# Value rows between the two page items of a slot, and the dot ahead of the score evacuation, in a decoder step on one core

## The reference, cut to what matters

```python
    s2 = jnp.einsum('btghd,btgnld->btghnl', q, ks).astype(jnp.float32) * scale      # selected scores
    o_slc = jnp.einsum('btghk,btgkd->btghd', p2.astype(vs.dtype), vs.reshape(...))   # selected values
...
    act = jax.nn.gelu(jnp.einsum('thkd,td->thk', u_tab[experts], xc))                # the dots
    v = v_tab[experts]
    return jnp.einsum('thk,thkd->td', (gate * act).astype(v.dtype), v)               # the value rows
```

## Time and profile before

| | |
|---|---|
| median of 3 runs | 2478.64 us (2475.55 to 2478.97) |
| the profiled execution | 2483.12 us, its span 2481.3 us |
| TensorE, matmul | 1764.9 us, 71% of the span |
| VectorE | 1271.6 us, 51% |
| ScalarE | 355.4 us, 14% |
| POOL | 847.4 us, 34% |
| DMA | 961.24 MB, mean 387 GB/s |
| granted TensorE clock, mean | 0.797 |

### The profile page before, as it was taken

How to read it: one execution, slowest core, us unless ns; L and a number is a source line. 1 busy time by engine, 2 the same in 40 slices (tenths; PEclk the granted TensorE clock), 3 DMA queues, 4 the chain that set the end, 5 groups by cost and what they waited for, 6 DMA issues and landing times.

```text
span 2481.3 us, 29990 instructions
## 1 busy us (share of the span) xinstructions
PE 1764.9 (71%) x9899; PEld 969.1 (39%) x9899; DVE 1271.6 (51%) x2384; ACT 355.4 (14%) x805; POOL 847.4 (34%) x595
## 2 busy tenths in 40 slices
PE   8999999979997787878665656769533333455335
PEld 6777766544696565556412213218200000000000
DVE  0500121253588775556959362345778754454651
ACT  0001110331230011110201020022200011021111
POOL 0000000000013443344324142332465677767662
PEclk9999999999998998889887778979655555555556
DMA  9999989997499999999999999999999999999997
GB/s 382 369 359 363 367 327 380 377 356 288 170 415 355 404 405 409 406 407 407 402 390 400 363 376 407 420 421 420 420 422 417 421 421 422 422 421 421 422 422 319
DMA packets 213309, 961.24 MB, mean 387 GB/s; under 512 B 23841, under 2 KB 89378, under 8 KB 122754
## 3 DMA queue, kind: packets, MB, share of 16 engines
q0 software_dynamic: 84432, 626.26, 61.4%
q1 hardware_dynamic: 92914, 300.39, 31.3%
q10 hardware_dynamic: 35808, 32.65, 3.9%
HBM read 952.73 MB, written 14.88 MB: 390 GB/s over the span
## 4 chain that ended last, share of the span: by engine, by line
DMA 46%; PE 39%; DVE 5%; issue 4%; ACTq 4%; POOL 1%; SPq 1%; ACT 1%; POOLq 0%; DVEq 0%
DMA sb<-in_peer_v,sb 24%; PE bank L1110 14%; DMA sb<-in_nsa_t 12%; PE bank L1531 6%; DMA sb<-in_peer_u,sb 5%; PE bank L1806 4%; PE bank L1417 3%; PE bank L1464 3%; PE bank L1181 2%; DMA sb<-in_nsa_v 2%; DVE sb L2480 2%; ACTq L440 2%; PE bank L1209 2%; DMA sb<-in_w_out 1%; DMA sb<-in_a_v 1%
## 5 line engine op out<-in xcount | busy, mean ns | idle before, releaser
L1806 PE MATMUL bank<-sb 128*32 128x512 f32 x2304 | 470.4, 867 | 495.8 <-DMA sb<-in_peer_v,sb 464.0
L2590 POOL DMA_INDIRECT sb<-in_peer_v,sb x288 | 497.3, 1727 | 576.1 <-PE bank L1806 510.9
L2480 DVE CUSTOM_DVE_ANT_1 sb<-sb 128x2048 f32<-128x2048 f32 x192 | 439.8, 2293 | 320.6 <-DMA sb<-in_peer_u,sb 317.4
L2590 POOL DMA_INDIRECT sb<-in_peer_u,sb x288 | 341.7, 1186 | 453.8 <-DVE sb L2480 241.1
L1806 PEld LDWEIGHTS bank<-sb 128*32 128x32 f32 x2304 | 60.7, 126 | 811.9 <-DMA sb<-in_peer_v,sb 741.6
L1110 PE MATMUL bank<-sb 128*128 128x288 f32 x1408 | 351.3, 409 | 7.5 <-DMA sb<-in_tokens_t 7.5
L1531 PE MATMUL bank<-sb 128*128 128x256 f32 x1024 | 280.2, 434 | 88.5 <-DMA sb<-in_nsa_t 79.6
L1110 PEld LDWEIGHTS bank<-sb 128*128 128x128 f32 x1408 | 265.8, 191 | 91.6 <-issue 13.0
L1531 PEld LDWEIGHTS bank<-sb 128*128 128x128 f32 x1024 | 249.3, 310 | 130.8 <-DMA sb<-in_nsa_t 93.8
L2480 DVE CUSTOM_DVE_ANT_0 sb<-sb 128x2048 f32<-128x2048 f32 x96 | 219.9, 2293 | 156.6 <-DMA sb<-in_peer_u,sb 154.9
L1069 ACT ACTIVATE sb<-sb 128x32 f32<-128x32 f32 x288 | 86.7, 316 | 725.0 <-PE bank L1806 428.9
(11 more groups left out here) (377 smaller groups left out, 1500.8 us busy)
## 6 DMA issues: line engine op xcount, KB each, us to landing
sb<-in_a_k SPq DMA_DIRECT2D x128, 512.0 KB, 7.4
sb<-in_a_v SPq DMA_DIRECT2D x128, 512.0 KB, 7.1
sb<-in_w_in SPq DMA_DIRECT2D x43, 1024.0 KB, 9.0
sb<-in_w_out SPq DMA_DIRECT2D x32, 1024.0 KB, 7.6
sb<-in_w_query SPq DMA_DIRECT2D x32, 1024.0 KB, 10.2
sb<-in_nsa_t SPq DMA_DIRECT2D x200, 128.0 KB, 11.8
sb<-in_nsa_t ACTq DMA_DIRECT2D x184, 128.0 KB, 15.2
sb<-in_nsa_v SPq DMA_DIRECT2D x64, 128.0 KB, 11.9
```

The lines of the kernel that those rows point to most:

```text
L1806: mm = pe.matmul(bank[g % 2][32 * c:32 * c + 32, :], diag[j % 4], rows[:, 512 * c:512 * c + 512], start=(s in FIRST), stop=(s in LAST), sk ...
L2480: dve.tensor_tensor_reduce(out=u, in0=u, in1=replica(g), scale=1.0, scalar=0.0, op0=ALU.mult, op1=ALU.add, accum_out=act16[:, r % 2, j:j + ...
L2590: pool.indirect_dma_start(rows[j % 4], None, dram[table], bass.IndirectOffsetOnAxis(ap=idx, axis=0)).then_inc(full[j % 4], 16)
```

## The change

TensorE: in the 16 slots with two selected items, `value_rows(t - 19)` moves from behind the second item to between the two (the list `SELECTED` takes these slots out of the common call at the loop's end). VectorE: in the slots 95, 97, 114 and 116, `gather_dot` moves ahead of `background`, so ahead of `slc_out` (and of `act_finish` in slot 114). Nothing is added or left out, no wait changes its value, and POOL, SP and ScalarE have the same programs as before.

```diff
--- before.py
+++ after.py
@@ -198,6 +198,7 @@
 
 
 ODD_PAGES = odd_page_ticks()
+SELECTED = {at + first + d for at in NSA_AT for first in (0, 13) for d in range(4)}
 OUT_AT = 132
 QUERY_AT = 146
 REPLICATE = {32 * (g - 1) + 20 + 2 * q: (g, q) for g in range(2, NGRP) if g != GROUPS_1 + 1 for q in range(4)}
@@ -1751,6 +1752,7 @@
                     d = t - NSA_AT[h]
                     if 0 <= d < 4:
                         selected_scores(h, 2 * d)
+                        value_rows(t - LAG)
                         selected_scores(h, 2 * d + 1)
                     elif d == 4:
                         new_scores(h)
@@ -1809,7 +1812,7 @@
 
             for t in range(SLOTS_ALL + LAG):
                 background(t)
-                if t >= LAG:
+                if t >= LAG and t not in SELECTED:
                     value_rows(t - LAG)
 
             for n in range(2):
@@ -2523,13 +2526,17 @@
             dve.wait_ge(saved, 1)
 
             for s in range(SLOTS_ALL):
+                waiting = any(s - at in (3, 5) for at in NSA_AT)
                 selection(s)
+                if waiting:
+                    gather_dot(s)
                 background(s)
                 if s in COLLECT:
                     collect(COLLECT[s])
                 if s >= 18 and s % 16 == 2:
                     act_finish(s // 16 - 1)
-                gather_dot(s)
+                if not waiting:
+                    gather_dot(s)
                 if s % 16 == 15:
                     act_start(s // 16)
             act_finish(2 * NGRP - 1)
```

## The result

| | us |
|---|---|
| changed kernel, median of 19 runs | 2483.14 (2476.96 to 2488.83) |
| kernel before, median of 19 runs beside them | 2477.82 (2473.1 to 2481.99) |
| ratio, 95% interval | 1.0019 [1.0012, 1.0025] |
| the profiled execution | 2483.45, its span 2481.7 |

The change costs 0.19%, 4.7 us at 2478. The forecast was 6.0 us saved, 2472.6 us, with a range up to 2481: the time is outside it and the sign is the other one. The difference is about as small as the 0.2% named there as what can be told from no change, but with 19 runs each the interval lies wholly above 1. A ratio here is not the quotient of the two medians; in the tables the two differ by up to 0.0011.

What follows compares the result with a forecast made beforehand. The prediction took the kernel to be bound by DMA moving bytes, with holes before 1700 us. Filling 3.4 + 3.5 + 0.6 less 1.5 of cost saved 6.0 us: from 2478.64 to 2472.6 us, range 2466.5 to 2481.

Steps and rivals of the forecast that it cites:

- What bounds the kernel: Whole kernel: it moves bytes, DMA holding 46% of the chain; a us saved ahead of 1700 us is kept.
- The holes and their filling: At 1418 to 1426 and 1454 to 1462 us, earlier v and u gathers fill DMA holes of 3.4 and 3.5 us.
- The size of the gain: From 1236 to 1560 us: holes total 8.8 us; 3.4 + 3.5 + 0.6 filled, less 1.5, gives 6.0 us saved.
- The step that failed: Second items used later, gathers sharing DMA with pages: cost 0.75 us at each of two score holes, bounds 0 and 7.7.
- The rule that I had weighed: Two page queues and one gather queue share DMA engines: item 1 estimated 1.8 us late, two places giving back 3.6 us.
- VectorE's half: Slots 95, 97, 114, 116: four dots, 9.2 us of VectorE, hidden in waits; nothing counted for it alone.
- The one on the other side: Rival, page chain binds: second items used later, successors loaded later, 1.93 us in each of four stretches, 2486.3 us; chance 0.09.
- The holes move: Rival: gathers come early but rings are empty again at the next point; 1.5 us saved, 2477 us; chance 0.33.

Runs made afterwards that it cites:

- the score slots alone: Against the kernel before: value rows between the two items only in slots 92 to 95 and 111 to 114, VectorE as before; 2488.97 us, ratio 1.0038.
- the value slots alone: Against the kernel before: value rows between the items only in slots 105 to 108 and 124 to 127; 2484.44 us, 1.0016, and again 2485.57 us, 1.0024.

## Why the prediction was wrong

**What bounds the kernel** held. The rate after 1700 us is 420 (419 before), and time lost ahead of it shows at the end.

**The holes and their filling** (3.4 and 3.5 us) held in part: value rows between the items, POOL's two issues 8.8 and 5.0 us earlier (forecast 11.7 and 9.5), 391 GB/s in 1400 to 1460 (forecast over 385), no hole at 1418 or 1454. But the stretch began 6.2 us late and TensorE did not wait for item 1, so that the filling there is partly the work of the delay ahead of it, which the forecast did not have. That the number over 385 came true is partly luck.

**The size of the gain** rested on one execution. A second one of the same kernel has 5.0 us of holes in place of 9.4 by one count (8.8 by the prediction's), and 326 and 399 GB/s at 1418 to 1426 where the earlier trace rows has 228 and 236; its two large holes lie at 1416 (294 GB/s) and 1448 to 1456 (312) and lack some 3 us together in place of 6.9. On the average of the two there were about 5 us to win there.

**The step that failed** is the cost: "The rows say that DMA is full at that time, so bytes are exchanged and not lost", 0.75 us for each score hole, and nothing for the first score stretch or for the value stretches. The exchange is not neutral, since pages and gathers aren't equally urgent. TensorE waits for pages; the rows it gathers early are for value rows a slot or more away. In place of the 1.5 us booked, the score slots alone came out 9 us slower and the value slots alone 4 to 6 us. Three of the four stretches took longer: 5 to 8 us between the first executions of both kernels (54.5 to 59.2, 49.6 to 58.0, 48.9 to 55.5), 7 to 11 between the second ones (51.4 to 62.3, 48.7 to 59.9, 49.0 to 55.6); the second score stretch got shorter (53.3 to 45.5 and 51.4 to 46.6). Behind such a stretch everything that hangs on the last item is late at a time when there are no pages left to fill the DMA engines. That the early gathers do it is shown for the score slots alone and for the value slots alone by holding them: 1.0038 to 1.0006 and 1.0024 to 1.0006; for the whole change it is not shown (1.0014 and 1.0013). By which chain the late last item costs time is read from the timelines: through the value rows right behind it, and through VectorE, whose dots hold the u gathers up to the next stretch. The VectorE half's 1.0038 to 1.0003 fits this and doesn't prove it.

The rule that I had weighed (the Trainium skill, "DMA: Bandwidth & Descriptors", section "Queues, rings and completion order": an engine goes round robin between the queues that have work) agrees in direction with the runs: pages come later when gathers share. No view here shows the packets' order itself. I had put it at an estimated 1.8 us for item 1; in the first score stretch item 1 was on time, item 2 came 3.9 us later behind item 0, and TensorE waited 7.7 us longer over the stretch.

**VectorE's half**: hidden, and nothing alone, as said (0.9997). To "count nothing for it alone" was right and not enough: together with the TensorE half it is worth 0.35% in the score slots alone, probably since it shortens the end of a stretch that the other half makes late.

**The rivals.** The one on the other side had the sign, and near the time (2486.3 against 2483.14), by another mechanism: it wanted the second item's buffer freed late, which costs 1.0007 [0.9996, 1.0017] when tried by itself. That its number came near is luck. *The holes move* was nearest in mechanism: they did, but behind the stretch, and by lengthening it, so that more than the gain was given back. It had been priced at 1.5 us of gain.

**Open.** The parts don't add up: 1.0038 and 1.0016 to 1.0024 apart, 1.0022 together (without the VectorE half). The second score stretch of both whole-change profiles is 45 to 47 us long, with the score slots alone it is 55.7, with the VectorE half added 47.3; which wait does it was not tried. Nor was the cause of the whole change's remaining 1.0013 with its gathers held.

## What to carry to other kernels

In a kernel bound by DMA, ask of every transfer that an edit makes earlier what it goes ahead of: while the engines are full a change of order does not show in the rate, and the price can come later, when the delayed consumer's chain leaves them empty. Look behind the end of such a stretch and at what hangs on its last item before booking the holes inside it. And take the size of holes from more than one execution, match a forecast's instruction by its place in the order and not by its time, and try two halves of an edit together as well as apart.

## What the runs showed that I had not expected

- With one gather pair of 2.1 MB (5.2 us at 405 GB/s) 12 us earlier against its stretch's start, the next item but one came 3.9 us later, TensorE waited 7.7 us longer for pages in that stretch, and the stretch took 11.5 us longer (one execution each); with the gathers held, all three were gone (21.6 us, 23.6 us and 52.6 us).
- The larger part of the loss stood behind the stretch and not in it: 317 GB/s from 1328 to 1352 us, where before moves 414 and 392.
- Two executions of one kernel, 2483.12 and 2476.59 us, differ by 4.4 us in holes (9.4 and 5.0) in a stretch of 324 us, so two thirds of the 6.5 us between these two arose here.
- Half a slot earlier or a whole one costs the same as far as these runs tell (1.0038 and 1.0039).
